# Sparse attention's scores ahead of its value products, which come in two parts, and low parts of weights ahead of the gates' scans

## The reference

```python
gq, gk, gv, glr, gg, nq, nkv, ngate = split_cols(h @ w_in, L1_SIZES)
log_a = jax.nn.log_sigmoid((glr @ w_gk2 + b_gk).astype(jnp.float32)) / GLA_GATE_NORM
o = gla_chunked(gq, gk, gv, log_a)            # bc = cumsum of log_a inside chunks of 64
o_gla = rmsnorm(o, gla_norm_g) * silu(gg)
# sparse attention, for each block of 128 queries and each of 8 heads
o_c = softmax(q @ k_cmp + bias, mask) @ v_cmp # compressed keys, 15 of them
o_s = softmax(q @ k_sel + bias, mask) @ v_sel # selected blocks (here all four)
o_w = softmax(q @ k_win + bias, mask) @ v_win # window of 512 (here all keys)
o_nsa = gate0 * o_c + gate1 * o_s + gate2 * o_w
return concat([o_gla, o_nsa]) @ w_out
```

## Time and profile before

| what | value |
|---|---|
| median of three runs | 2024.4 us (2017.91, 2024.4, 2027.9) |
| the profiled execution's own time | 2022.43 us |
| its span, first to last instruction | 2020.6 us |
| mean granted TensorE clock | 0.976 |
| busy share of the span: PE, DVE, ACT, POOL | 94%, 69%, 49%, 13% |
| stretch of the gates' stage touched by the change | some 463 to 489 us |
| stretch of sparse attention's two query blocks | some 636 to 710 us |

### The profile page before, as it was taken

The page is one execution under the profiler, slowest core; times in us unless marked ns, Lnnn a source line. Parts: engine busy times, 40 slices in busy tenths (PEclk is TensorE's granted clock), DMA queues, the critical chain, the costliest instruction groups (busy, mean ns, idle before and its releaser), DMA issues.

```text
span 2020.6 us, 33216 instructions
## 1 busy us (share of the span) xinstructions
PE 1906.9 (94%) x13188; PEld 1758.9 (87%) x13188; DVE 1392.5 (69%) x2530; ACT 986.9 (49%) x1432; POOL 256.6 (13%) x118
## 2 busy tenths in 40 slices
PE   6899799989998889998999899999999999999998
PEld 6887699979977679998998889999998888999997
DVE  5897765557966674336757548988878887666665
ACT  5545544454435354445555445566653334444444
POOL 0001044430001024440000057000000000000000
PEclk8999899999989899999999999999999999999999
DMA  8653466655555245555444344577766865555452
GB/s 315 240 185 135 152 246 241 236 197 207 200 194 191 73 152 193 188 188 187 153 146 167 125 153 163 174 217 216 215 217 233 314 238 218 205 213 203 172 202 111
DMA packets 94232, 392.79 MB, mean 194 GB/s; under 512 B 7648, under 2 KB 41584, under 8 KB 55552
## 3 DMA queue, kind: packets, MB, share of 16 engines
q1 hardware_dynamic: 94080, 390.69, 55.5%
HBM read 372.83 MB, written 15.73 MB: 192 GB/s over the span
## 4 chain that ended last, share of the span: by engine, by line
PE 76%; DVE 13%; ACT 2%; issue 2%; DMA 1%; POOL 0%; DVEq 0%; SPq 0%; ACTq 0%
PE ps L563 10%; PE ps L564 10%; PE ps L565 10%; PE acc L559 9%; PE acc L560 9%; PE acc L561 9%; PE acc L563 3%; PE acc L564 3%; PE acc L565 3%; DVE wlo L1295 2%; PE ps L1250 1%; PE acc L1250 1%; DVE arena L1324 1%; PE acc L852 1%; PE ps L629 1%
## 5 line engine op out<-in xcount | busy, mean ns | idle before, releaser
L2343 ACT ACTIVATE whi<-raw 128x1024 fp32r<-128x1024 f32 x559 | 590.9, 1060 | 498.1 <-PE acc L561 275.2
L1295 DVE TENSOR_TENSOR wlo<-raw,whi 128x1024 fp32r<-128x1024 f32 x463 | 571.4, 1241 | 296.7 <-ACT whi L2343 293.9
L563 PE MATMUL ps<-hhi,whi 128*128 128x256 f32 x1824 | 524.2, 287 | 12.9 <-ACT hhi L2457 6.3
L564 PE MATMUL ps<-hlo,whi 128*128 128x256 f32 x1824 | 519.7, 285 | 0.0
L565 PE MATMUL ps<-hhi,wlo 128*128 128x256 f32 x1824 | 519.6, 285 | 0.0
L563 PEld LDWEIGHTS ps<-hhi,whi 128*128 128x128 f32 x1824 | 353.4, 194 | 19.0 <-ACT hhi L2457 7.3
L564 PEld LDWEIGHTS ps<-hlo,whi 128*128 128x128 f32 x1824 | 353.4, 194 | 2.9
L565 PEld LDWEIGHTS ps<-hhi,wlo 128*128 128x128 f32 x1824 | 353.3, 194 | 0.0
L1295 POOL TENSOR_TENSOR wlo<-raw,whi 128x1024 fp32r<-128x1024 f32 x96 | 239.1, 2493 | 631.8 <-ACT whi L2343 631.5
L559 PE MATMUL acc<-whi,chi 128*128 128x512 f32 x752 | 295.7, 393 | 3.5 <-DVE wlo L1295 1.9
L560 PE MATMUL acc<-whi,clo 128*128 128x512 f32 x752 | 294.3, 391 | 0.0
(11 more groups left out here) (446 smaller groups left out, 2383.1 us busy)
## 6 DMA issues: line engine op xcount, KB each, us to landing
raw<-in_peer_down SPq DMA_DIRECT2D x64, 1024.0 KB, 5.0
raw<-in_peer_up SPq DMA_DIRECT2D x64, 1024.0 KB, 5.2
arena<-in_ada SPq DMA_DIRECT2D x80, 512.0 KB, 5.3
raw<-in_w_gate SPq DMA_DIRECT2D x22, 1024.0 KB, 4.8
raw<-in_w_up SPq DMA_DIRECT2D x22, 1024.0 KB, 4.8
raw<-in_w_down SPq DMA_DIRECT2D x22, 1024.0 KB, 4.8
arena<-spill SPq DMA_DIRECT2D x14, 1024.0 KB, 7.2
spill<-hT_t SPq DMA_DIRECT2D x22, 448.0 KB, 6.4
```

Of the source, the lines that this page charges most:

```text
L563: e.matmul(out, hi, xh, start=start, stop=False, skip_group_check=True)
L564: e.matmul(out, hi, xl, start=False, stop=False, skip_group_check=True)
L1295: e.tensor_tensor(out=lo, in0=w, in1=hi.bitcast(F32), op=ALU.subtract).then_inc(*X(("lo", j)))
L2343: e.activation(hi, w, ACT.Copy, scale=1.0).then_inc(*self.A(("hi", j)))
```

## The change

In the gates' stage ScalarE cuts the high parts of g4 and g5 between Exp and Ln, and VectorE their low parts in front of L1793 and the scans. In sparse attention `pe_nsa` issues the scores of a (qt, br) step at the end of the step before it. The value products become a function. Those of qt = 0 are issued in step (1, 0), behind its part of `w_out1a` and ahead of its transposes; VectorE's and ScalarE's splits of that bank move to the same place. Those of qt = 1 come in two parts: compressed keys and branch 0 ahead of the last transposes, which have three banks for that time, and branch 1 at the end. Only the first product into the bank has start set. The first two score groups, of (0, 0), stay where they were; the number of matmuls does not change.

```diff
+    def pe_nsa_heads(self, e, qt, branches):
+        m = self.m
+        if 0 in branches:
+            e.wait_ge(*self.at("out", "pct", qt))
+        for br in branches:
+            self.pe_turned(e, f"nsa{qt}{br}", 8, 128 * (qt + 1))
+        ps = self.banks.take(e, f"nsa{qt}", "heads") if 0 in branches else self.banks.tile(f"nsa{qt}", "heads")
+        for j in range(4):
+            if 0 in branches:
+                e.matmul(ps[:, j * 128:(j + 1) * 128], m.vb[:, 2 * j:2 * j + 2, :].rearrange("p a d -> p (a d)"), m.pct,
+                         start=j == 0, stop=False, skip_group_check=True)
+            for g in range(2):
+                for br in branches:
+                    for kt in range(qt + 1):
...
+        if 1 in branches:
+            t.then_inc(*self.P(("full", f"nsa{qt}", "heads")))
...
+        self.pe_cmp_scores(e, 0)
+        self.pe_nsa_scores(e, 0, 0)
         for qt in range(2):
...
                 self.pe_out(e, "w_out1a", range(at, at + 2), m.cH, m.cL, at == 0, False, "mix1_post", "gla", ada=False)
+                if (qt, br) == (1, 0):
+                    self.pe_nsa_heads(e, 0, (0, 1))
+                elif (qt, br) == (1, 1):
+                    self.pe_nsa_heads(e, 1, (0,))
+                    self.banks.order = [b for b in ROT if b != self.banks.of["nsa1", "heads"]]
                 self.pe_turn(e, f"nsa{qt}{br}", 8, nk, m.St1)
                 if br == 0:
...
+                    self.pe_nsa_scores(e, qt, 1)
+                elif qt == 0:
+                    self.pe_cmp_scores(e, 1)
+                    self.pe_nsa_scores(e, 1, 0)
+        self.pe_nsa_heads(e, 1, (1,))
+        self.banks.order = ROT
...
                 self.ve_ada(e)
+                self.ve_cuts(e, "w_gqk", 31)
                 e.wait_ge(*self.at("log_gate"))
...
                                ahead=self.W.last("w_out1a", 2 * at + 1, 512) + 2)
+                if (qt, br) == (1, 0):
+                    self.ve_bank_split(e, "nsa0", m.hH, m.hL, 0)
                 self.ve_out_by_rows(e, "w_out1a", range(at, at + 2), ada=False)
...
-            self.ve_bank_split(e, f"nsa{qt}", m.hH, m.hL, qt)
+        self.ve_bank_split(e, "nsa1", m.hH, m.hL, 1)
...
                 e.activation(m.bcum, m.bcum, ACT.Exp, scale=-1.0).then_inc(*A())
+                self.se_cuts(e, "w_gqk", 31)
                 e.wait_ge(*A.last)
...
                 self.se_scores(e, f"nsa{qt}{br}", 8, nk, m.St1)
+                if (qt, br) == (1, 0):
+                    self.se_bank_split(e, "nsa0", m.hH, 0)
                 self.se_out(e, "w_out1a", range(at, at + 2))
...
-            self.se_bank_split(e, f"nsa{qt}", m.hH, qt)
+        self.se_bank_split(e, "nsa1", m.hH, 1)
```

More of the change, by code:

```diff
@@ L1030, in pe_cmp_turn, with pe_cmp_scores, pe_nsa_scores, score @@
         t.then_inc(*self.P(("full", "cmp_turn", kind)))
+    def pe_cmp_scores(self, e, qt):
+        m = self.m
+        for g in range(2):
+            ps = self.banks.take(e, "cmp_scores", qt, g)
+            for j in range(4):
+                t = e.matmul(ps[:, 16 * j:16 * j + 16], m.nq[64 * g:64 * g + 64, j, qt * 128:(qt + 1) * 128],
+                             m.kcm[64 * g:64 * g + 64, :], start=True, stop=True, skip_group_check=True)
+            t.then_inc(*self.P(("full", "cmp_scores", qt, g)))
+    def pe_nsa_scores(self, e, qt, br):
+        m = self.m
+        nk = 128 * (qt + 1)
+        def score(out, s):
+            r = 64 * (s % 2)
+            return e.matmul(out, m.nq[r:r + 64, s // 2, qt * 128:(qt + 1) * 128], m.ksw[r:r + 64, br, 0:nk], start=True,
+                            stop=True, skip_group_check=True)
+        self.pe_scores(e, f"nsa{qt}{br}", 8, nk, score)
+    def pe_nsa_heads(self, e, qt, branches):
+        m = self.m
+        if 0 in branches:
[3 more added lines that the diff above has]
+        ps = self.banks.take(e, f"nsa{qt}", "heads") if 0 in branches else self.banks.tile(f"nsa{qt}", "heads")
+        for j in range(4):
+            if 0 in branches:
+                e.matmul(ps[:, j * 128:(j + 1) * 128], m.vb[:, 2 * j:2 * j + 2, :].rearrange("p a d -> p (a d)"), m.pct,
+                         start=j == 0, stop=False, skip_group_check=True)
+            for g in range(2):
+                for br in branches:
+                    for kt in range(qt + 1):
+                        t = e.matmul(ps[64 * g:64 * g + 64, j * 128:(j + 1) * 128],
+                                     m.vsw[:, kt, 128 * br + 64 * g:128 * br + 64 * g + 64],
+                                     m.PT1[br][:, kt, 2 * j + g, :], start=False, stop=br == 1 and kt == qt,
+                                     skip_group_check=True)
+        if 1 in branches:
+            t.then_inc(*self.P(("full", f"nsa{qt}", "heads")))
     def pe_nsa(self, e):
```

12 lines of the change are left out of this document (removed).

## The result

The changed kernel took 2002.56 us (median of five runs, 2001.0 to 2004.56); the kernel before took 2020.1 us (median of five, 2017.91 to 2027.9, the three of its table among them), so 17.5 us less. The ratio of the means is 0.9905, 95% interval 0.9882 to 0.9927. The forecast of 2008.0 lies 5.4 us above the median. The profiled execution took 2001.54 us of its own time; its span is 1999.8 us, 20.8 less than before's 2020.6.

A forecast was written before the change was run, and what follows sets the result against it. TensorE's waits (76% of the chain) and lower clock in two stretches bound the kernel. Gains of 4.0 and 11.4 make 15.4 us, taking the profiled 2022.4 to 2007.0; forecast median 2008, range 2002 to 2016.

The forecast's parts named there:

- part two: Sparse attention: reordered scores and value products fill TensorE's gaps; 11.4 us gained, 8.3 from order, 3.1 from clock falls.
- footing: Whole kernel: the starting time, median 2024.4 us before, from which the forecast median of 2008 was set.
- handing on: Behind the gate rows: what later stages gain from the earlier start, priced at nothing.
- Part one: Gates' stage: earlier cuts remove 3.16 us of stall and 1.7 of clock, add 0.8 of stall; 4.0 us gained.
- four times 0.42 and half of 1.5, 4.7 us: Sparse attention, qt = 1: time for value products of compressed keys and branch 0 at full clock.
- branch 1 takes 3.0: Sparse attention, qt = 1: the last value products take 3.0 us, ending at 696.5 against 708.05.
- gate rows start 15 us earlier: End of sparse attention: sign of being right, gate rows start 15 us earlier than 709.7.
- clock rival: Both stretches: clock keeps falling in the denser order, costing 4.8 or 1.7 us; 2010 to 2013; chance 0.20.
- 3.1 us that I credited to removed falls: Sparse attention: share of the 11.4 us from two clock falls with no long gap before them any more.
- Part one does not do what it says: Gates' stage: TensorE's wait merely moves from g4 to g6, leaving 2012 us; chance 0.09.
- little arrives: Whole kernel: a later stage gives the gain back, by transfer or clock; 2014 to 2024 us; chance 0.08.
- slower: Sparse attention: clock falls at the first new gap and stays low, 18 us later; end 2036; chance 0.03.

The follow-up runs named there:

- e2: Changed kernel without the gates' cuts (sparse-attention part alone): 2008.25 us, ratio to the kernel before 0.9932.
- e3: Changed kernel with the value products of qt = 1 in one piece behind the last transposes, four banks again: 2008.08 us.
- e4: Changed kernel with the value products of qt = 0 and their splits ahead of the scores of (1, 0) again: 2008.95 us.
- e5: Changed kernel plus 14 unread matmuls of 512 columns in TensorE's gap ahead of the first transposes of (0, 0): 2000.26 us.
- e9: e5 plus 28 transposes of the identity ahead of the norm's transposes at four places: 1999.78 us.
- e10: e9 plus 12 more transposes of the identity behind the norm's transposes at three places: 2002.34 us.
- e12: Changed kernel with no edit, profiled and timed a second time: 2003.50 us, ratio to the kernel before 0.9907.
- e1: Kernel before with the gates' cuts alone: 2013.88 us, ratio to the kernel before 0.9963.
- e11: Kernel before with all the fills of e10: 2016.24 us, ratio to the kernel before 0.9977.

## Why the prediction was right in its reasons and 5.4 us too high

The step that failed is a term of part two's sum: the value products of qt = 1 at the old rate, 7.7 us for 5.94 measured. Behind it stand two things outside the sum of the parts: the median of three runs as footing, and handing on, put at nothing, where the profiles have 4.3 us outside both stretches. The bullets take them in turn.

- **Part one, forecast 4.0, measured 3.97.** Every sign it named came: L1821 begins at 469.45, 0.57 behind L694 (forecast 471.9, 0.76 behind 471.14); no gap behind L694; 0.70 before g6 for 0.8. The one flaw is in its reading: it booked 1.7 us of clock as removed for certain. e2 shows the same wait without a fall, so 2.5 is the order's share. By e2 that fall was worth 1.5 us, not 1.7.
- **Part two, forecast 11.4, measured 12.56 by the starts of the rows.** From the end of the transposes of (0, 1), as the prediction measures it, it is 35.1 us (652.87 to 687.97) for 36.2 forecast. The step that failed is the value products: "four times 0.42 and half of 1.5, 4.7 us" and "branch 1 takes 3.0" are 3.95 and 1.99 in the trace, together 1.8 us less. The other way went the start of step (1, 0): from 652.87 to the products' end at 665.75 it took 12.88 us for 12.4, 0.5 more, of which the scores are 0.4 (652.87 to 656.16 is 3.29; I had 2.9). By the first value product of qt = 1, at 677.42, the new order ran 0.8 us behind the forecast (24.55 us for 23.75), so the 1.1 us of the whole are 1.8 less 0.8 and a rest of 0.1. The reading of the order itself was right: e3 and e4 bring back each its own gaps. The sign "gate rows start 15 us earlier" came as 21.7, of which 16.5 lie in the two stretches and 5.2 in places ahead of and between them.
- **The footing.** 4.3 of the 5.4 us are no term of the sum. I set 16.4 us of gain (2024.4 less 2008; the sum had 15.4) against the median of three runs, 2024.4; five runs gave 2020.1, and the medians of before beside the experiments are 2020.4 to 2022.0. Against 2020.1 the same gain gives 2003.7. With three values 10 us apart, the middle one is no footing to half a per cent.
- **The clock rival (0.20) is refuted in its place.** Gaps of 0.77, 1.00 and 1.61 us brought no fall in the changed stretches: PEclk is 1.00 from 653 to 684, and attention is 36.06 to 36.10 in the six profiles with this very order (after, e2, e5, e9, e10, e12). The Trainium skill's rule that small idles between groups of matmuls can make the clock go to and fro ("TensorE: Matmul & The Clock Gate", section "A second HAM failure mode: psum-queue depth-cycling") is not borne out at these sizes. Part of the 3.1 us that I credited to removed falls was luck of before's execution, though: before's order took 48.62, 47.17 (e1) and 46.40 (e11). Against the mean of the three, 47.4, part two is worth 11.3. At an even clock it is some 9.4, an estimate: the prediction's arithmetic puts the old order with only the first fall at 706.5, which is 45.45 behind 661.05. So the forecast of 11.4 comes so near to 11.3 because two errors cancel: the products made it 1.8 us too small, and the falls taken for sure made it too large.
- **Handing on was priced at nothing, and 4.3 us came.** From profile to profile the gain is 20.8 us, 16.5 in the two stretches and 4.3 outside both; behind the gate rows after is 0.90 us slower. The 4.3 us lie beside a shorter half clock: leaving out the 3.4 and 10.2 us that went in the changed stretches, 22.5 of the 36.1 us are left, at 0.25 us each (e12) 5.6 us. That the clock is the cause of all 4.3 is argued from this, not shown. By the medians less is left for it: 17.5 less 16.5 is 1.0, and less 15.3 (4.0 and 11.3) it is 2.2. The prediction did price the clock ("one fall of 3.4 us is worth 1.7"), at 0.5 us a microsecond; measured are 0.25 to 0.32 over a whole execution and 0.4 in the two stretches that show it.
- "Part one does not do what it says", "little arrives" and "slower" didn't occur; nothing in the traces leans to them.

Best seen: e5 and e9, after with the fills, at 2000.3 and 1999.8 us. They beat before clearly (0.9886 and 0.9898), and after by 2 to 3 us, where the intervals overlap. e5 needs 14 wasted matmuls at one place and is the simpler one.

What stays open: why the length of a fall differs between executions of one kernel, what gave the 4.3 us outside the two stretches, and whether e5's 2.3 us last. What was not tried is a wait taken out ahead of the first transposes of (0, 0) by an earlier start of that step's scores, which is the one long gap (3.36 us) left in sparse attention.

## What to carry to other kernels

Where two engines take turns on one chain (scores, softmax, products), look for work of a later step that needs nothing of the chain's last link, and put it into the wait; read the gain off as the sum of gaps that then have work in them, and name what fills each. When a loop is cut in pieces, don't carry the old duration of a matmul over: ask which matmuls are now neighbours, and into which half of a bank they write. And separate the kernel's part from the clock's: a stretch between two fixed rows repeated here within 0.1 us where no fall lay in it, while whole executions of one kernel differed by 8 (after) to 15 (before).

## What the runs showed of the hardware that I had not expected

- Instructions that write 64 rows of a bank take 62 ns each in turns of two or four a half and 103 in sixteens, in the last group of 32; with products of all 128 rows between the groups it is 75 in fours, 94 in eights and 102 in sixteens.
- After one and the same wait of about 3.4 us the granted clock was half for 10.2, 6.8 or 0 us; after the 3.16 us ahead of g4, for 3.4 (before, e11) or 0 (e2). A shorter wait doesn't rule a fall out: in e3 the wait ahead of the first transposes was 1.75 us, and T holds a fall as in after (11.48 us).
- A VectorE product of 128x8 that began 0.1 us behind a GpSimd instruction took 2.32 us and not 0.17.
- A microsecond at half clock goes with 0.25 us of time (after) or 0.32 (before) over a whole execution, and cost 0.4 in a stretch where TensorE had no long wait behind it (T: 6.8 us of fall, 2.8 us of time; the gates: 3.4 and 1.5).
